# The memory norm's gain moved into the key and value weights, and the raw memory tiles turned as they land

## The reference, cut to what matters

```
def rms_norm(x, g):
    y = xf * lax.rsqrt(jnp.mean(xf * xf, axis=-1, keepdims=True) + EPS)
    return (y * g.astype(jnp.float32)).astype(x.dtype)

mkv = rms_norm(mem, mem_norm_g) @ w_mem_kv          # per layer; mem is the same for both
m_k, m_v = jnp.split(mkv, 2, axis=-1)
k_c = rms_norm(split_heads(m_k, CA_HEADS), ca_k_g)
```

## Time and profile before

| | |
|---|---|
| time, median of 3 | 1546.23 us (1545.79 to 1547.57) |
| span of the profiled execution | 1544.4 us |
| TensorE busy | 1500.5 us, 97% |
| VectorE, ScalarE, GpSimd busy | 555.6, 430.9, 83.0 us |
| mean granted TensorE clock | 0.994 |
| HBM over the span | 310 GB/s |

### The profile page before, as it was taken

How to read it: one execution, slowest core, us unless ns; L and a number is a source line. 1 busy time by engine, 2 the same in 40 slices (tenths; PEclk the granted TensorE clock), 3 DMA queues, 4 the chain that set the end, 5 groups by cost and what they waited for, 6 DMA issues and landing times.

```text
span 1544.4 us, 30813 instructions
## 1 busy us (share of the span) xinstructions
PE 1500.5 (97%) x13934; PEld 937.8 (61%) x13934; DVE 555.6 (36%) x672; ACT 430.9 (28%) x551; POOL 83.0 (5%) x126
## 2 busy tenths in 40 slices
PE   8999999999999999999999999999999999998877
PEld 7788888788888887887335353353433533534224
DVE  5755576655567655666400101011010110010101
ACT  6557654544445567554000000000000000000000
POOL 5211100000002111001000000000000000000000
PEclk9999999999999999999999999999999999999999
DMA  7555454665665555678999999999999999999996
GB/s 275 178 152 166 148 166 152 229 188 175 204 189 183 177 147 155 213 291 313 418 398 405 420 426 430 428 427 428 428 427 430 429 426 428 426 431 427 428 428 252
DMA packets 86242, 480.38 MB, mean 311 GB/s; under 512 B 11296, under 2 KB 13408, under 8 KB 64096
## 3 DMA queue, kind: packets, MB, share of 16 engines
q1 hardware_dynamic: 84480, 474.67, 79.3%
q0 software_dynamic: 1632, 3.74, 0.8%
HBM read 477.34 MB, written 1.05 MB: 310 GB/s over the span
## 4 chain that ended last, share of the span: by engine, by line
PE 84%; DMA 11%; DVE 2%; POOL 2%; issue 1%; ACT 0%; SPq 0%; DVEq 0%; POOLq 0%
PE pa L2128 26%; PE ps L2128 18%; PE pa L1998 13%; PE pa L2000 12%; PE pa L1999 12%; DMA exp_raw<-in_moe_slabs 11%; DVE w_lo L1292 1%; DMA w_raw<-in_w_mem_kv 1%; POOL hrs L805 1%; POOL head_gains L734 0%; PE ps L1914 0%; PE ps L2301 0%; PE ps L2122 0%; PE pa L2033 0%; PE ps L2278 0%
## 5 line engine op out<-in xcount | busy, mean ns | idle before, releaser
L2128 PE MATMUL pa<-exp_raw,xf 128*32 128x512 f32 (+1 forms) x5104 | 492.1, 542 | 19.5 <-DMA exp_raw<-in_moe_slabs 17.0
L2128 PEld LDWEIGHTS pa<-exp_raw,xf 128*32 128x32 f32 x5104 | 163.7, 110 | 325.7 <-issue 267.1
L1292 DVE TENSOR_TENSOR w_lo<-w_raw,w_hi 128x1024 fp32r<-128x1024 f32 x226 | 274.2, 1232 | 121.8 <-ACT w_hi L930 112.9
L930 ACT ACTIVATE w_hi<-w_raw 128x1024 fp32r<-128x1024 f32 (+1 forms) x228 | 236.9, 1053 | 146.3 <-PE pa L2000 144.8
L2128 PE MATMUL ps<-exp_raw,hf 128*32 128x256 f32 x4384 | 246.0, 383 | 10.0 <-DMA exp_raw<-in_moe_slabs 8.4
L1998 PE MATMUL pa<-w_hi,r 128*128 128x512 f32 x600 | 239.8, 400 | 1.2 <-DVE r L1327 1.1
L2000 PE MATMUL pa<-w_hi,r 128*128 128x512 f32 x600 | 233.9, 390 | 0.0
L1999 PE MATMUL pa<-w_lo,r 128*128 128x512 f32 x600 | 233.9, 390 | 0.0
L1859 DVE TENSOR_TENSOR hs<-pa,hs 128x768 f32<-128x768 f32 (+3 forms) x32 | 23.7, 742 | 584.2 <-ACT hs L1255 584.2
L2128 PEld LDWEIGHTS ps<-exp_raw,hf 128*32 128x32 f32 x4384 | 144.5, 111 | 114.6 <-issue 13.0
L1255 ACT ACTIVATE hs<-pa 128x768 f32<-128x768 f32 (+3 forms) x32 | 20.4, 637 | 661.0 <-PE pa L2128 661.0
(11 more groups left out here) (280 smaller groups left out, 816.3 us busy)
## 6 DMA issues: line engine op xcount, KB each, us to landing
exp_raw<-in_moe_slabs SPq DMA_DIRECT2D x82, 3072.0 KB, 33.0
exp_raw<-in_moe_slabs SPq DMA_DIRECT2D x87, 1024.0 KB, 8.2
w_raw<-in_w_in SPq DMA_DIRECT2D x104, 512.0 KB, 4.4
w_raw<-in_ff_w_gate_up SPq DMA_DIRECT2D x44, 512.0 KB, 4.5
w_raw<-in_ff_w_down SPq DMA_DIRECT2D x22, 512.0 KB, 4.2
w_raw<-in_w_mem_kv SPq DMA_DIRECT2D x16, 512.0 KB, 5.3
w_raw<-in_w_out SPq DMA_DIRECT2D x16, 512.0 KB, 4.2
w_raw<-in_w_br_sb SPq DMA_DIRECT2D x8, 512.0 KB, 3.7
```

The source lines that it names most:

```text
L930: act.activation(dst, raw, ACT.Copy).then_inc(hi_ready, 1)
L1292: dve.tensor_tensor(dst, raw, hi.bitcast(F32), ALU.subtract)\
L2128: return pe.matmul(dst, a, b, start=start, stop=stop, skip_group_check=True)
```

## The change

The 512 KB broadcast of the memory gain is gone. SP loads both layers' gains as 16 rows of 128 numbers instead; TensorE turns these into columns (`gain_columns` in PSUM), VectorE copies them to `mem_gain`. When a slab of mem_k or mem_v is split, in both layers, each of its two halves of 512 columns belongs to one block of 128 memory columns and is multiplied by that block's gain, a scale per partition: two instructions on each engine in place of one. The memory tiles land in `tok` and `sq` and are turned raw, with no wait for VectorE; for layer 1 too, where the squares and the normalisation of the memory fall away, and `mem_rstd` of layer 0 is used again at the readout. In `x_norm` of layer 0 ScalarE squares x before it splits slabs 2 and 3, and the memory after that; GpSimd takes x's roots, then the memory's. GpSimd loads the mixer's gain when memory tile 1 has landed. The first product's first slab is done tile by tile. TensorE's idle turns are 6, 2 and 9 in place of 12 and 6.

```diff
         @block.sync
-            sp.dma_start(hn[:, 0, :], memory_in[:, 0, :]).then_inc(first_tile[0], 16)
-            sp.dma_start(gain[:, :], mem_norm_g[0].rearrange("(o d) -> o d", o=1)
-                         .broadcast_to([P, DM])).then_inc(first_gain, 16)
-            sp.dma_start(hn[:, 1, :], memory_in[:, 1, :]).then_inc(first_tile[1], 16)
+            sp.dma_start(start_x[0], memory_in[:, 0, :]).then_inc(first_tile[0], 16)
+            sp.dma_start(mem_rows[:, :], mem_norm_g.rearrange("l (k p) -> (l k) p", p=P))\
+                .then_inc(mem_rows_loaded, 16)
+            sp.dma_start(start_x[1], memory_in[:, 1, :]).then_inc(first_tile[1], 16)
...
+        def gain_halves(s):
+            for p in table:
+                if p.name in ("mem_k", "mem_v") and p.first <= s < p.end:
+                    per = SLAB // p.width
+                    k = p.layer * KT + (s - p.first) * per
+                    return [(slice(n * p.width, (n + 1) * p.width), mem_gain[:, k + n:k + n + 1])
+                            for n in range(per)]
+            return []
...
         @block.gpsimd
-                load_gain(1)
-                inverse_root(mem_rstd)
+                pool.wait_ge(first_tile[1], 16)
+                load_gain(0)
...
             def memory(l):
-                inverse_root()
-                load_gain(3 * l + 1)
                 yield
                 yield
             def x_norm(l):
                 inverse_root()
                 if l == 0:
+                    inverse_root(mem_rstd)
                     mixer_constants()
-                load_gain(3 * l + 2)
+                load_gain(2 * l + 1)
...
         @block.scalar
+                for cols, scale in gain_halves(s):
+                    if s == 0:
+                        act.wait_ge(mem_gain_ready, 1)
+                    ins = act.activation(dst[:, cols], raw[:, cols], ACT.Copy, scale=scale)
...
             def start():
                 splits_until(2)
-                for t in range(NT):
-                    act.wait_ge(first_tile[t], 16)
-                    square(hn, t)
             def memory(l):
-                act.wait_ge(mem_reloaded, 16)
-                for t in range(NT):
-                    square(hn, t)
                 yield
...
             def x_norm(l):
                 if l == 0:
-                    splits_until(4)
                     act.wait_ge(x_loaded, 16)
-                    act.wait_ge(norm_rs, NT)
                 for t in range(NT):
-                    square(xs, t)
+                    square(xs[:, t, :], t)
+                if l == 0:
+                    splits_until(4)
+                    act.wait_ge(norm_rs, NT)
+                    for t in range(NT):
+                        act.wait_ge(first_tile[t], 16)
+                        square(start_x[t], t)
...
         @block.vector
+                    for cols, scale in gain_halves(s):
+                        ins = dve.scalar_tensor_tensor(out=dst[:, cols], in0=raw[:, cols],
+                                                       scalar=scale, in1=hi[:, cols].bitcast(F32),
+                                                       op0=ALU.mult, op1=ALU.subtract)
...
             def start():
-                    dve.tensor_tensor(start_x[t], hn[:, t, :], gain[:, :], ALU.mult)\
-                        .then_inc(norm_done, 1)
+                dve.wait_ge(mem_rows_turned, 1)
+                dve.tensor_copy(mem_gain[:, :], gain_columns).then_inc(mem_gain_ready, 1)
...
             def x_norm(l):
+                nonlocal norms
+                for t in range(NT):
+                    mean_square(t)
+                if l == 0:
+                    splits_until(3)
+                    dve.wait_ge(x_loaded, 16)
+                else:
+                    dve.wait_ge(turn_ready, turns)
+                for t in range(NT):
+                    normalise(xs, t, l)
                 if l == 0:
                     splits_until(4)
+                    for t in range(NT):
+                        mean_square(t)
+                    norms += NT
...
         @block.tensor
             def start():
                 pe.wait_ge(consts, 1)
-                idle_turns(12, 0)
-                for t in range(NT):
-                    turn_tokens(True, ps, t, True)
                 idle_turns(6, 0)
+                pe.wait_ge(mem_rows_loaded, 16)
+                pe.matmul(gain_columns, mem_rows[:, :], ident[0:LAYERS * KT, 0:LAYERS * KT],
+                          start=True, stop=True).then_inc(mem_rows_turned, 1)
+                idle_turns(2, 0)
+                for t in range(NT):
+                    turn_tokens(False, ps, t, True)
+                idle_turns(9, 0)
...
+                        if p is table[0] and g == 0:
+                            for t in range(NT):
+                                pe.wait_ge(turn_lo, t + 1)
+                                ins = multiply(0, [t])
```

More of the change, by code:

```diff
@@ L236, in trunk @@
             cum_tri = early("cum_tri", [P, P])
+            mem_rows = early("mem_rows", [LAYERS * KT, P])
+            mem_gain = early("mem_gain", [P, LAYERS * KT])
         exp_raw = sb("exp_raw", [P, EXP_RAW, EXP_SLAB])
@@ L329, in trunk @@
         first_tile = [sem("mem_tile0_loaded"), sem("mem_tile1_loaded")]
-        mem_reloaded, first_gain = sem("mem_reloaded"), sem("first_gain")
+        mem_reloaded, mem_rows_loaded = sem("mem_reloaded"), sem("mem_rows_loaded")
+        mem_rows_turned, mem_gain_ready = sem("mem_rows_turned"), sem("mem_gain_ready")
         x_loaded, gain_loaded, gains_loaded = (sem(n) for n in (
@@ L709, in link @@
                 pool.wait_ge(pool_step, steps)
-            gain_order = [g[l] for l in range(LAYERS) for g in (mem_norm_g, mix_norm_g, ffn_norm_g)]
+            gain_order = [g[l] for l in range(LAYERS) for g in (mix_norm_g, ffn_norm_g)]
             def load_gain(k):
-                pool.wait_ge(norm_done, NT * k)
+                if k > 0:
+                    pool.wait_ge(norm_done, NT * k)
                 pool.dma_start(gain[:, :], gain_order[k].rearrange("(o d) -> o d", o=1)
@@ L787, in ffn_norm @@
                 inverse_root()
-                load_gain(3 * l + 3)
+                load_gain(2 * l + 2)
                 pool.wait_ge(turn_ready, NT * TURNS * (l + 1))
@@ L927, in split @@
                 dst, raw = w_hi[:, s % SPLIT, 0:n], raw_slot(s)[:, 0:n]
+                for cols, scale in gain_halves(s):
+                    if s == 0:
+                        act.wait_ge(mem_gain_ready, 1)
+                    ins = act.activation(dst[:, cols], raw[:, cols], ACT.Copy, scale=scale)
+                if gain_halves(s):
+                    ins.then_inc(hi_ready, 1)
+                    return
                 if n < SLAB:
@@ L1006, in ffn_norm @@
                 act.wait_ge(taken["rows"], residual("out", l, 1))
-                square(xs, 1)
+                square(xs[:, 1, :], 1)
             def route_left(t, turns):
@@ L1020, in edge @@
                     act.wait_ge(taken["rows"], residual("out", p.layer, 0))
-                    square(xs, 0, last_out(p))
+                    square(xs[:, 0, :], 0, last_out(p))
                 elif first_out(p) and at == "tile1":
@@ L1044, in product @@
                 l = p.layer
-                first_memory = l == 0 and p.name in ("mem_k", "mem_v")
+                of_memory = p.name in ("mem_k", "mem_v")
+                first_memory = l == 0 and of_memory
                 if first_memory:
-                    act.wait_ge(norm_rs, NT)
+                    act.wait_ge(norm_rs, NT * 2)
                 def root(t):
@@ L1051, in root @@
                         return nrstd[:, t:t + 1]
-                    return mem_rstd[:, t:t + 1] if first_memory else 1.0
+                    return mem_rstd[:, t:t + 1] if of_memory else 1.0
                 if p.name == "ff_gate":
@@ L1232, in _ @@
             act.wait_ge(taken["rows"], residual("out", LAYERS - 1, 1))
-            square(xs, 1, True)
+            square(xs[:, 1, :], 1, True)
             route_copy(1)
@@ L1288, in splits_until @@
                     hi = w_hi[:, s % SPLIT, 0:w]
+                    for cols, scale in gain_halves(s):
+                        ins = dve.scalar_tensor_tensor(out=dst[:, cols], in0=raw[:, cols],
+                                                       scalar=scale, in1=hi[:, cols].bitcast(F32),
+                                                       op0=ALU.mult, op1=ALU.subtract)
+                    if gain_halves(s):
+                        ins.then_inc(lo_ready, 1)
+                        done += 1
+                        continue
                     if w < SLAB:
@@ L1346, in start @@
                 splits_until(2)
-                for t in range(NT):
-                    mean_square(t)
-                norms += NT
             def memory(l):
[L1352 to L1356, removed]
                 yield
@@ L1908, in turn_tokens @@
                     enter()
```

(11 more changed lines are left out.)

20 lines of the change are left out of this document (10 added, 10 removed).

## The result

The changed kernel takes 1553.67 us (median of five, 1551.4 to 1554.43) against 1546.77 us before: ratio 1.0044, 95% interval 1.0032 to 1.0056. It is slower by 6.9 us, outside the range of 1544.7 to 1549.8. Two executions far out of the rest, one of the kernel before (1910 us) and one of clock_kept (6525 us), are left out of every time given here.

A forecast was written before the change was run, and what follows sets the result against it. GpSimd's in-order list was taken as the bound: starting 1.6 us later, it moves the profiled span from 1544.4 to 1546.0; the median lies 1.8 us above the profiled span, so 1547.8 us, range 1544.7 to 1549.8.

The forecast's parts named there:

- What bounds the kernel: First 70 us: GpSimd's in-order list; its delay costs its full size, a gain of TensorE alone is worth nothing.
- the new order: GpSimd's list starts behind the memory's roots in place of x's, the last roots of the start with the change.
- the sum from split 2 to the mean squares: ScalarE and VectorE: split 2 done at 15.6, then lower halves 2 and 3 and x's normalisations, to 20.7.
- The front of the transfers: SP's queue at the start: removed broadcast gives 1.3 us, GpSimd's gain load takes back 0.3; x at 12.3.
- squares of x much off 12.3: Sign on ScalarE that the prediction would be wrong: x's squares starting much off 12.3 us.
- T: Time at which VectorE begins the memory's mean squares: 20.7 us, 19.9 to 21.7 by the bounds.
- The roots: GpSimd's two memory roots alternate with VectorE's lower halves; the list starts at T+3.3, 24.0 against 22.38, 1.6 us later.
- rival B: GpSimd gets in only when VectorE pauses: list starts at 25.7, 3.3 us late; 1549.5 us; chance 0.10.
- The clock: TensorE's 3.6 us wait before the mem_k heads may withhold 1.7 us; 1.6 us slack at 69.5 pays, nothing added.
- Behind the head scores: Layer 1 and later slabs: TensorE's queue of split slabs hides the halves; 3.6 us at most if that failed.

The follow-up runs named there:

- clock_kept: The changed kernel with 20 idle TensorE turns in its wait before the turns of the mem_k heads; 1552.67 us, ratio 1.0044.
- gain_later: The changed kernel with GpSimd loading the mixer's gain when slab 0 has landed in place of memory tile 1; 1552.03 us, ratio 1.0039.
- roots_free: The changed kernel with VectorE starting lower half 4 only when the memory's two roots are taken; 1548.83 us, ratio 1.0014.
- roots_behind: The changed kernel with GpSimd taking the memory's roots after the mixer constants in place of before them; 1547.90 us, ratio 1.0009.
- broadcast_back: gain_later with the 512 KB broadcast of the memory gain put back behind memory tile 0, its data not used; 1552.64 us.
- no_halves: The changed kernel with whole, unscaled splits of the memory's slabs, the memory gain left out; 1551.57 us, ratio 1.0032.
- first_halves: The changed kernel with halves and scales for layer 0's mem_k alone, the other 12 memory slabs split whole and unscaled; 1552.51 us, ratio 1.0035.

## Why the prediction was wrong

**What bounds the kernel** was right. A late start of GpSimd's list is carried to the end at its full size: a_up starts 5.7 us late, the mem_k heads are turned 5.7 us late, and each run that moved a_up moved the head scores and the end with it: a_up at 28.1, scores at 76.2, span 1551.9 in the changed kernel; 26.5, 73.8 and 1550.2 in gain_later; 24.4, 71.7 and 1547.3 in roots_free; 22.4, 69.5 and 1544.4 before. At 17.5 (roots_behind) the readout had taken over. TensorE's own path was not last in the changed kernel. Also right was the new order, the list behind the memory's roots, and the sum from split 2 to the mean squares: 18.36 to 23.41 is 5.05 us, predicted 5.1.

**The front of the transfers failed.** I put x at 12.3, by 1.3 us that the removed bytes would give and 0.3 that the gain load would take. x was there at 14.9, and the prediction had named squares of x much off 12.3 as a sign of being wrong. broadcast_back shows that the removal gave at most 0.3 us: I had divided bytes by the 399 GB/s of 7 to 14 us and applied that to the front, where the queue moved 229 to 291. The early load costs 0.8 on average, and x was 1.6 later in the profiled execution than in gain_later's: 0.3 was a choice out of 0 to 1.3, for which no row spoke. The Trainium skill, page "DMA: Bandwidth & Descriptors", section "Issuing engines are not separate DMA queues", was weighed at this point and pointed the right way: GpSimd's load interleaves with SP's, and the runs agree, x being 0.8 us earlier on average with the later load. With x late by 2.6 us T moves from 20.7 to 23.41, 2.7 us.

**The roots failed: rival B came true.** I let roots and splits alternate, so that the list starts at T + 3.3. It started at T + 4.7 (23.41 to 28.11); rival B had T + 4.9 and the same sequence: the first root after three splits, the second beside the lower halves that read PSUM. I had read the pair at 74 us as an alternation. It shows only that a split waited for one GpSimd instruction and that the next one waited for the split, behind which VectorE paused. No row showed GpSimd getting in between two splits, and rival B, which had a chance of 0.10, should have been the forecast. The range ended at B with x on time; no case had both. The Trainium skill, page "SBUF — State Buffer", section "Who interferes with whom", has the two exclude each other for whole instructions; the trace agrees, with a root that ended 0.42 us after the third split. In all six profiles in which the roots stand beside three splits (the changed kernel, gain_later, broadcast_back, clock_kept, no_halves, first_halves) the pair took 4.35 us. roots_free prices the hold at 3.2 us.

**The clock was under-sized.** I took the wait before the heads for 3.6 us and its low clock for 1.7 us of work, covered by TensorE's slack of 1.6. The wait was 5.6, and the clock withheld 2 x (0.50 + 0.50 + 0.50) = 3.0 us from 46 to 52, with TensorE at work from 46.12 on. From the turns to the scores TensorE took 30.1 us, against 29.1 before with the wait of 1.6 in it, so 2.6 us more. The slack paid 1.6 of them and 1.0 came on top (6.7 at the scores against 5.7 at the heads); in clock_kept's execution 0.8 of it is gone. That it came out at 1.0 is a matter of the execution: with a like wait it was nothing in three others.

**Behind the head scores** I counted nothing, and 0.8 us came on top, in two jumps of 0.35 to 0.4 between 176 and 209 us and between 627 and 660 us of the kernel before. no_halves and roots_free don't have them, and roots_free has all the halves; their cause stays open.

The terms add up: 1.6 predicted, 2.7 for x, 1.4 for the roots, 1.0 for the clock and 0.8 behind it, together 7.5 us, as the spans differ. They are the terms of the two profiled executions; with x's average landing the second would be 0.7 smaller. With x at 14.9 and rival B the prediction's own steps give 1547.8 + 2.6 + 1.6 = 1552.0; the rest up to 1553.7 is the clock and what lies behind the scores.

## What to carry to other kernels

Before moving a step, ask what is queued behind it on its engine: two roots of half a microsecond carried 20 DMA issues and a chain of 48 us with them (a_up at 28.11 to the scores at 76.22). Work that reads data which lands early belongs where its engines idle at that time: the same change with the memory's squares at the landing was faster than the kernel before. And a short GpSimd instruction put beside a run of VectorE instructions with two SBUF inputs can cost the whole run, not one of them: here a root of 0.56 us waited out three splits and took 3.73.

## What was not expected of the hardware

From 4 to 8 us the changed kernel moves 229 to 291 GB/s in stretches of 2 us, and 390 to 425 from 8 to 12, although less stands at the head of the queue than before; x's landing varied by 1.9 us (9.8 to 11.7 after its issue) over seven kernels whose queue starts alike. In the kernel before x was squared 5 us after it had landed (13.3 and 18.30); in the changed kernel it heads the chain, and its spread may be why the five executions after span 3.0 us and the five before 1.8, which no run shows.
